# A long split-precision transformer kernel: eight units after the first and after the last RMS norm multiply unscaled tiles, and their results are scaled in the PSUM bank

## The chip, the cores and the metric

One NeuronCore of a Trainium2 chip runs the whole program. The metric is the device time of one execution in microseconds (us). Engines: TensorE (PE in the profile; PEld is its weight load), VectorE (DVE), ScalarE (ACT), GpSimd (POOL), SyncE (SP, which here issues every DMA).

## The reference

Input x is 256 tokens by 1024 features, f32. A first block is followed by two layers of a second kind:

```python
# first block
h = rms_norm(x, norm_mix_g); proj = h @ w_in            # 8192 columns
# eight attention heads, four differential heads, a gated linear recurrence,
# three gates; each branch through its own matrix, gated, summed
x = x + merged @ w_out
x = x + ffn(rms_norm(x, norm_ffn_g))                    # 2 * 2816 columns, conv, gelu
x = rms_norm(x, final_norm_g)
# then, twice
proj = x @ w_in_2[l]                                    # pool, q, k, v, conv, gates
x = layer_norm(ALPHA * x + merged @ w_o_2[l]); x = layer_norm(ALPHA * x + ffn(x))

def rms_norm(x, g):
    return x * rsqrt(mean(x * x, -1) + 1e-6) * g
```

The root depends on the token alone, the gain g on the feature alone. Features lie on the partitions here, so g is a column operand, and 1/root has to be a row that is the same on every partition.

## The kernel before

All activations are kept transposed: a tile is 128 features by S = 256 tokens, and x has KT = 8 tiles. A **unit** is one block of 128 output columns: its weight is 128 x 1024 (eight 128 x 128 blocks). f32 precision is kept by splitting: ScalarE writes `whi` (`hi_part`, line 716), VectorE writes `wlo` = raw - whi (`lo_part`, line 1372), and in `product_of` (lines 1048 to 1050) TensorE makes three matmuls for each block, whi x xhi, whi x xlo, wlo x xhi: 24 in a unit. Weights come by DMA into a ring of RING = 3 slots (`load`, line 499, on SP, which waits until the slot's `wlo` has been made). A unit's result lies in one of three banks, `unit_bank[r % 3]`, and `begin` waits until the result three before has been read (`FREE`).

The order on each engine is written out by hand. Stage `win1` has 64 units; after unit n ScalarE copies its bank to SBUF (lines 900, 897, 906), and `steps(n)` issues `hi_part(n + 3)`, on VectorE `lo_part(n + 3)`, and the small steps that `schedule` puts in slot n: `prepare_*` (tiny VectorE work), `rg_gates`, `rg_scan`, `scores` (DVE line 1541, softmax on ACT line 798), `weights` (transposes on PE line 1200, copy on ACT line 810), `values` (PE line 1220). The engines run their own lists in order and meet only at semaphores. After win1 come merge1, wout1, up1, down1, then per layer win2, wout2, up2, down2.

The two norms in question:

- The first (`first_rms`, `rms("mix", ...)`). Squares of x on ACT (line 765) and DVE (line 1453), sums over tiles on POOL (`add_squares`, line 644), sums over partitions on PE (`token_sums`, line 1105), root on ACT (line 727), reciprocal and diagonal on DVE (lines 1386, 1381), spread to all partitions by a matmul with ones (`spread_out`, line 1111). Then DVE makes the scaled tiles `dev` (line 1409), ACT `xhi` (line 758), DVE and POOL `xlo` (lines 1376, 650), and `ramp` lets units 0 and 1 start tile by tile. PE fills waits with `warm`, matmuls on ones (line 1064).
- The final (`rms("final", ...)`), after the last unit of down1 and before win20: the same, with squares made during down1 (line 931) from the residual (line 1691), `x` scaled in place.

Of the kernel before, what the change touches and what calls it, by code (L numbers as in the profile page):

```python
# [10 lines left out]
S = 256  # L11
# [13 lines left out]
RING = 3  # L25
# [6 lines left out]
PLAN1 = sum([[t, 24 + t] for t in range(KT)], []) + list(range(8, 24)) + list(range(32, WIN1))  # L32
# [102 lines left out]
def schedule():  # L135
# [5 lines left out]
    for n, name in enumerate(("prepare_scalars", "prepare_exps", "prepare_series", "prepare_sum", "prepare_softplus")):  # L141
        at(1 + n, name)
    for t in range(KT):
        at(6 + 2 * t, "rg_gates", t)
    at(22, "rg_roots",)
    for t in range(KT):
        at(23 + t, "rg_input", t)
        at(24 + t, "rg_scan", t)
        at(48 + t, "rg_hidden", t)
        at(49 + t, "rg_split", t)  # L150
    for half in range(NQT):
        at(21 + half, "turn_v", 0, half)
        at(33 + half, "turn_v", 1, half)
# [12 lines left out]
    for h in range(DIFF_H):  # L166
        at(53 + 2 * h, "diff_spread", h)
        at(54 + 2 * h, "diff_norm", h)
        at(55 + 2 * h, "diff_low", h)
    for l in range(LAYERS2):  # L170
        b = START[f"win2{l}"]
        at(b + 2, "rope", l, 0)
        at(b + 3, "turn_v2", l)
        for i in range(4):
            at(b + 4 + i, "rope", l, 1 + i)
        for pair in range(4):
            w = MOBA_H + DIFF_H + 8 * l + 2 * pair
            at(b + 9 + 4 * pair, "scores", MOBA_H // 2 + DIFF_H + 4 * l + pair)
            for i in range(2):
                at(b + 12 + 4 * pair + i + (pair == 2), "weights", w + i)  # L180
            at(b + 14 + 4 * pair + (pair == 2), "values", w)
# [10 lines left out]
SLOTS = schedule()  # L192


def build(nc, args, out):
# [3 lines left out]
    with ctx:  # L199
# [69 lines left out]
        def cst(name, n):  # L269
# [12 lines left out]
        load_vec, load_const, load_rg, load_pos, load_ident = (  # L282
            sem(n) for n in ("load_vec", "load_const", "load_rg", "load_pos", "load_ident"))
# [13 lines left out]
        normed_dve, normed_act, x_hi, x_lo, x_lo_pool = (sem(n) for n in ("normed_dve", "normed_act", "x_hi", "x_lo", "x_lo_pool"))  # L297
# [122 lines left out]
        def bank_of(r):  # L420
            return unit_bank[r % 3]

# [35 lines left out]
        FIRST_SUMMED = KT - 2  # L458
        ACCQ = {n: FIRST_SUMMED - 1 + (KT - 2) * (i - 1) if i else 0 for i, n in enumerate(NORMS)}
# [4 lines left out]
        POOL_LOW = (4, 6)  # L464
# [10 lines left out]
        for n in NORMS:  # L475
            for t in range(KT):
                if n not in LNI:
                    NORMED[n, t] = tell(normed_dve)
                elif n == NORMS[-1]:
                    NORMED[n, t] = tell(normed_dve if dve_last(t) else normed_act)  # L480
                if n != NORMS[-1]:
                    LOW[n, t] = tell(x_lo_pool if n not in LNI and t in POOL_LOW else x_lo)
# [7 lines left out]
        def _(sp):  # L490
            for i in range(KT // 2):
                sp.dma_start(x[:, 2 * i:2 * i + 2, :], args["x"][:, 2 * i:2 * i + 2, :]).then_inc(load_x[i], 16)
            def load(n, it=0, per=0):
# [18 lines left out]
            sp.dma_start(rgw[:], args["rg_w"]).then_inc(load_rg, 16)  # L512
# [1383 lines left out]
```

## Time and profile before

| what | us |
|---|---|
| median of 3 runs | 1244.67 (1243.55 to 1249.49) |
| the profiled execution | 1243.38 |
| its span in the trace | 1241.6 |
| PE busy | 1216.5 |
| DVE, ACT, POOL busy | 851.7, 706.1, 400.0 |

The span is what the trace covers; the 1.8 us beside it lie around it. A row of the timeline is: start, duration (of a merged run: of the whole), engine, line, operation, output<-input, shapes, count, and in brackets the engine's idle time before it with what ended that. Starts of consecutive rows give the pace; durations of pipelined matmuls overlap. Rows of the windows give busy time and number of instructions per engine, and PEclk, the clock that TensorE was granted (1.00 is 2.4 GHz, 0.50 is 1.2 GHz).

### The profile page before, as it was taken

To read this page: it belongs to the slowest core of one execution; us is meant where nothing else is said; L and a number is where in the kernel's file an instruction comes from. 1 tells how busy PE (TensorE), PEld (TensorE's weight loads), DVE (VectorE), ACT (ScalarE), POOL (GpSimd) and SP (SyncE) were. 2 spreads that over 40 slices of the span, in tenths; PEclk is the share of its full clock that TensorE was granted. 3 is DMA by queue.
4 is the path that set the end of the run, shared out by engine and by line. 5 is a ranking of instruction groups with operands and counts; after the bars stand their busy time and mean duration, and the time that the engine had idled before them with its cause. 6 is when DMAs were issued, how large, how long until landed. Compare 5 with 4: busy or idle time off the path is not lost. (4 is left out here: it accounts for less than half of the span.)

```text
span 1241.6 us, 27228 instructions
## 1 busy us (share of the span) xinstructions
PE 1216.5 (98%) x10224; PEld 1192.8 (96%) x10224; DVE 851.7 (69%) x1458; ACT 706.1 (57%) x1228; POOL 400.0 (32%) x376
## 2 busy tenths in 40 slices
PE   8999999999999999999999999999999999999997
PEld 8998889999999999999999999999999999999997
DVE  6858665676777755766667777756766677777755
ACT  5676666545766654466445666644466445666642
POOL 2007204023343401210338443314610339343313
PEclk9999999999999999999999999999999999999999
DMA  7554445655665666454554666664554554665662
GB/s 257 187 160 150 132 136 153 189 187 154 181 190 187 191 192 179 153 164 144 186 171 135 184 186 189 184 187 155 153 169 148 177 175 131 187 188 187 192 193 88
DMA packets 60288, 212.70 MB, mean 171 GB/s; under 512 B 6688, under 2 KB 7968, under 8 KB 60064
## 3 DMA queue, kind: packets, MB, share of 16 engines
q1 hardware_dynamic: 60192, 211.39, 55.8%
q8 instruction: 65, 1.06, 0.4%
q14 instruction: 31, 0.25, 0.1%
HBM read 210.31 MB, written 1.05 MB: 170 GB/s over the span
## 5 line engine op out<-in xcount | busy, mean ns | idle before, releaser
L1372 DVE TENSOR_TENSOR wlo<-raw,whi 128x1024 fp32r<-128x1024 f32 (+1 forms) x400 | 493.8, 1235 | 298.7 <-ACT whi L716 296.2
L1048 PE MATMUL bank<-xhi,whi 128*128 128x256 f32 x2240 | 636.6, 284 | 6.0 <-DVE wlo L1372 3.6
L1049 PE MATMUL bank<-xlo,whi 128*128 128x256 f32 x2240 | 624.4, 279 | 0.0
L1050 PE MATMUL bank<-xhi,wlo 128*128 128x256 f32 x2240 | 624.4, 279 | 0.0
L716 ACT ACTIVATE whi<-raw 128x1024 fp32r<-128x1024 f32 (+1 forms) x400 | 415.7, 1040 | 154.1 <-PE bank L1050 148.2
L1048 PEld LDWEIGHTS bank<-xhi,whi 128*128 128x128 f32 x2240 | 421.8, 188 | 16.5 <-issue 7.2
L1049 PEld LDWEIGHTS bank<-xlo,whi 128*128 128x128 f32 x2240 | 422.6, 189 | 0.6
L1050 PEld LDWEIGHTS bank<-xhi,wlo 128*128 128x128 f32 x2240 | 422.2, 188 | 0.0
L617 POOL TENSOR_TENSOR fprod<-ugate,uval 128x256 f32<-128x256 f32 x66 | 93.3, 1414 | 212.1 <-DVE uval L1717 206.5
L1048 PE MATMUL bank<-fhi,whi 128*128 128x256 f32 x528 | 148.0, 280 | 0.0
L1050 PE MATMUL bank<-fhi,wlo 128*128 128x256 f32 x528 | 147.7, 280 | 0.0
L1049 PE MATMUL bank<-flo,whi 128*128 128x256 f32 x528 | 147.6, 280 | 0.0
L631 POOL TENSOR_TENSOR u<-u,tmp 128x256 f32<-128x256 f32 x48 | 53.6, 1117 | 240.4 <-DVE tmp L1672 239.2
L1048 PE MATMUL bank<-yhi,whi 128*128 128x256 f32 x384 | 108.4, 282 | 0.0
L1050 PE MATMUL bank<-yhi,wlo 128*128 128x256 f32 x384 | 107.8, 281 | 0.0
L1049 PE MATMUL bank<-ylo,whi 128*128 128x256 f32 x384 | 107.8, 281 | 0.0
L1050 PEld LDWEIGHTS bank<-fhi,wlo 128*128 128x128 f32 x528 | 100.4, 190 | 0.0
L1049 PEld LDWEIGHTS bank<-flo,whi 128*128 128x128 f32 x528 | 99.4, 188 | 0.1
L1048 PEld LDWEIGHTS bank<-fhi,whi 128*128 128x128 f32 x528 | 99.1, 188 | 0.1
L976 ACT ACTIVATE fhi<-fprod 128x256 f32 (+1 forms) x66 | 27.6, 418 | 81.0 <-POOL fprod L617 81.0
L1048 PEld LDWEIGHTS bank<-yhi,whi 128*128 128x128 f32 x384 | 72.8, 189 | 0.3
L1050 PEld LDWEIGHTS bank<-yhi,wlo 128*128 128x128 f32 x384 | 73.0, 190 | 0.0
(201 smaller groups left out, 1287.8 us busy)
## 6 DMA issues: line engine op xcount, KB each, us to landing
raw<-in_w_win SPq DMA_DIRECT2D x140, 512.0 KB, 3.6
raw<-in_w_up SPq DMA_DIRECT2D x132, 512.0 KB, 3.6
raw<-in_w_down SPq DMA_DIRECT2D x48, 448.0 KB, 3.6
raw<-in_w_merge SPq DMA_DIRECT2D x32, 512.0 KB, 4.1
raw<-in_w_out SPq DMA_DIRECT2D x24, 512.0 KB, 3.5
raw<-in_w_down SPq DMA_DIRECT2D x24, 512.0 KB, 3.5
x<-in_x SPq DMA_DIRECT2D x4, 256.0 KB, 3.9
rgw<-in_rg_w SPq DMA_DIRECT2D x1, 1024.0 KB, 10.0
```

The costliest lines, as they stand in the source:

```text
L617: pool.tensor_tensor(tile(fprod, t % 3), tile(ugate, t % 3), tile(uval, t % 3), ALU.mult).then_inc(product, 1)
L631: ins = pool.tensor_tensor(m, m, branch_part(base, t, branch), ALU.add)
L716: act.activation(whi[:, n % RING, 0:blocks * P], raw[:, n % RING, 0:blocks * P], ACT.Copy).then_inc(split_hi, 1)
L976: act.activation(tile(fhi, t, it, 3), tile(fprod, t % 3), ACT.Copy).then_inc(f_hi, 1)
L1048: pe.matmul(ps, whi[:, slot, w], hi, start=first, stop=False)
L1049: pe.matmul(ps, whi[:, slot, w], lo, start=False, stop=False)
L1050: return pe.matmul(ps, wlo[:, slot, w], hi, start=False, stop=last)
L1372: dve.tensor_tensor(wlo[:, n % RING, w], raw[:, n % RING, w], whi[:, n % RING, w].bitcast(f32), ALU.subtract) \
```

## The change

RAW_UNITS = 8 units of win1 and of win20 no longer wait for the norm. They multiply x times the gain (`raw_high` on ACT, `raw_low` on DVE, into free halves of yhi and ylo); when the root is known, `copy_inverse` puts the spread row in SBUF and `scale_raw` on DVE multiplies each of the eight results in its bank, before ACT copies it (`unit_ready`). Three more banks (`SPARE`: ps_score, ps_turn, ps_stat) hold results 3 to 5. The sums go through PE after unit 2 (first norm) or unit 0 (final), the spread after the next unit. The scaled tiles are still made, by `normal`, `norm_hi`, `low_part`, `gained_low`, and in the first norm partly on POOL, between those units, for unit 8 on. `hi_part`/`lo_part` of units 3 to 5 (first) and 3, 4 (final) are issued ahead, and `AHEAD` says where the others go. POOL adds all eight square tiles. The first loads come in another order, with the gain column alone first. The order of win1's units changes (columns of the recurrence now begin at unit 8), and `schedule` moves nearly every small step of win1: prepare 1..5 to 7..11, rg_gates from 6 to 12, rg_roots 22 to 27, scores from every third unit from 25 to every second from 29, the differential heads' values from one unit after their weights to two. In win20 the rope steps come four units later, the attention steps one.

The diff, cut to its core:

```diff
-PLAN1 = sum([[t, 24 + t] for t in range(KT)], []) + list(range(8, 24)) + list(range(32, WIN1))
+RAW_UNITS = 8
+PLAN1 = list(range(8)) + sum([[24 + t, 8 + t] for t in range(KT)], []) + list(range(16, 24)) + list(range(32, WIN1))
...
-    at(22, "rg_roots",)
+        at(12 + 2 * t, "rg_gates", t)
+    at(27, "rg_roots",)
...
-        at(25 + 3 * pair, "scores", pair)
+        at(29 + 2 * pair, "scores", pair)
         for i in range(2):
-            at(27 + 3 * pair + i, "weights", 2 * pair + i)
-        at(29 + 3 * pair, "values", 2 * pair)
+            at(31 + 2 * pair + i, "weights", 2 * pair + i)
+        at(33 + 2 * pair, "values", 2 * pair)
     for h in range(DIFF_H):
-        at(36 + 2 * h, "scores", MOBA_H // 2 + h)
-        at(39 + 2 * h, "weights", MOBA_H + h)
-        at(40 + 2 * h, "values", MOBA_H + h)
-    at(47, "rg_gelu",)
-    at(48, "diff_sums",)
-    at(49, "diff_recip",)
+        at(37 + 2 * h, "scores", MOBA_H // 2 + h)
+        at(40 + 2 * h, "weights", MOBA_H + h)
+        at(42 + 2 * h, "values", MOBA_H + h)
...
+AHEAD = {0: 0, 1: 0, 2: 4, 3: 4, 4: 4, 5: 0, START["win20"]: 0, START["win20"] + 1: 0}
...
+        RAW_STAGE = {"mix": "win1", "final": "win20"}
+        GAIN = {"mix": "norm_mix_g", "final": "final_g"}
+        RAWI = {n: i for i, n in enumerate(RAW_STAGE)}
+        SPARE = {RESULT[name] + i: (ps_score, ps_turn, ps_stat)[i - 3] for name in RAW_STAGE.values() for i in range(3, 6)}
+        raw_xhi, raw_xlo = yhi[:, 0:KT, :], ylo[:, 0:KT, :]
+        inverse_rows = tmp[:, 2, :]
+        def bank_of(r, it=0):
+            if isinstance(it, int) and r in SPARE:
+                return SPARE[r]
             return unit_bank[r % 3]
+        def raw_units(which, i, it=0):
+            return which in RAWI and i < RAW_UNITS and isinstance(it, int)
...
+        ADDS = {n: KT - 1 if n in RAWI else KT - 2 for n in NORMS}
+        ACCQ = {n: sum(ADDS[m] for m in NORMS[:i]) for i, n in enumerate(NORMS)}
...
+            sp.dma_start(vec[:, 0:KT], args["vec"][:, 0:KT]).then_inc(load_gain, 16)
+            for i in (0, 1):
+                load_pair(i)
             load(0)
+            for i in (2, 3):
+                load_pair(i)
+            load(1)
             sp.dma_start(ident, args["const"][:, 0:P]).then_inc(load_ident, 16)
-            sp.dma_start(vec[:], args["vec"]).then_inc(load_vec, 16)
-            for n in range(1, RING):
+            load(2)
+            load(3)
+            sp.dma_start(vec[:, KT:], args["vec"][:, KT:]).then_inc(load_vec, 16)
+            for n in (4, 5):
...
+            pool.wait_ge(inverse_copied, 1)
+            for t in range(4, KT):
+                pool.tensor_tensor(dev[:, t, :], x[:, t, :], inverse_rows, ALU.mult).then_inc(normed_pool, 1)
             low_parts("mix", dev)
...
+            def raw_high(which, t, it=0):
+                if which != "mix":
+                    wait(act, res_new, RES[which] + t + 1, it, 2)
+                act.activation(tile(raw_xhi, t, it, 2), tile(x, t, it, 2), ACT.Copy, scale=gained(which, t, it)).then_inc(raw_hi, 1)
+            def copy_inverse(which):
+                act.wait_ge(spread, SUM[which])
+                act.activation(inverse_rows, spread_inverse, ACT.Copy).then_inc(inverse_copied, 1)
+            def unit_ready(which, i, n, it=0, per=0):
+                if raw_units(which, i, it):
+                    act.wait_ge(raw_scaled, RAW_UNITS * RAWI[which] + i + 1)
+                else:
+                    wait(act, unit_done, n + 1, it, per)
...
+            def first_square(t):
                 act.activation(dev[:, t, :], x[:, t, :], ACT.Square).then_inc(squared, 1)
+            for half in range(2):
+                for t in range(4 * half, 4 * half + 4):
+                    if t % 2 == 0:
+                        act.wait_ge(load_x[t // 2], 16)
+                    raw_high("mix", t)
+                if half == 0:
+                    first_square(0)
+                    first_square(2)
+                hi_part(half)
+            first_square(4)
+            first_square(6)
+            hi_part(2)
+            hi_part(3)
+            hi_part(4)
             norm_root("mix", RMS_EPS)
-            hi_part(0)
-            norm_hi("mix", dev, {3: 1})
-            hi_part(2)
+            copy_inverse("mix")
+            hi_part(5)
...
+                if n < 4:
+                    norm_hi("mix", dev, (2 * n, 2 * n + 1))
...
+            hi_part(START["win20"] + 2)
             norm_root("final", RMS_EPS)
-            hi_part(START["win20"] + 2)
-            norm_hi("final", x)
+            hi_part(START["win20"] + 3)
+            copy_inverse("final")
+            hi_part(START["win20"] + 4)
...
-                if result is not None and result >= banks:
+                if result is not None and result >= banks and not (isinstance(it, int) and result in SPARE):
...
+            def rms_sums(which):
+                token_sums(square_sums, [(acc[:, 0, :], added_q, ACCQ[which] + ADDS[which])]).then_inc(summed, 1)
+            def rms_spread(which):
                 pe.wait_ge(inverted, SUM[which])
                 spread_out(spread_inverse, 1).then_inc(spread, 1)
-                warm(7, 0)
+            def raw_unit(which, i):
+                name = RAW_STAGE[which]
+                n, r = START[name] + i, RESULT[name] + i
+                sums = 2 if which == "mix" else 0
+                ready = [(raw_lo, KT * RAWI[which] + k + 1) for k in range(KT)] if i == 0 else None
+                plain(n, r, bank_of(r)[:, 0:S], ready=ready, split=(raw_xhi, raw_xlo))
+                if i == sums:
+                    rms_sums(which)
+                if i == sums + 1:
+                    rms_spread(which)
...
+            def scale_raw(which, i):
+                n, ps = START[RAW_STAGE[which]] + i, bank_of(RESULT[RAW_STAGE[which]] + i)[:, 0:S]
+                if i == 0:
+                    dve.wait_ge(inverse_copied, RAWI[which] + 1)
+                dve.wait_ge(unit_done, n + 1)
+                dve.tensor_tensor(ps, ps, inverse_rows, ALU.mult).then_inc(raw_scaled, 1)
+                dve.wait_ge(raw_scaled, RAW_UNITS * RAWI[which] + i + 1)
+            def gained(which, t, it=0):
+                a = COLS[GAIN[which]] + t
+                return vec[:, a:a + 1] if isinstance(it, int) else vec[:, bass.ds(it * 2 + a, 1)]
+            def raw_low(which, t, it=0):
+                wait(dve, raw_hi, KT * RAWI[which] + t + 1, it, 2)
+                dve.scalar_tensor_tensor(tile(raw_xlo, t, it, 2), tile(x, t, it, 2), gained(which, t, it), tile(raw_xhi, t, it, 2).bitcast(f32),
+                                         ALU.mult, ALU.subtract).then_inc(raw_lo, 1)
...
+                    raw_low("mix", t)
+                if half == 0:
+                    first_square(1)
+                    first_square(3)
+                lo_part(half)
+            first_square(5)
+            first_square(7)
+            lo_part(2)
+            lo_part(3)
+            lo_part(4)
             dve.wait_ge(load_ident, 16)
-            rms("mix", "norm_mix_g", dev, 0, (6, 1))
-            lo_part(2)
+            invert("mix")
...
+                    scale_raw("mix", n)
+                    if n < 2:
+                        normal("mix", dev, (2 * n, 2 * n + 1))
+                    if n == 0:
+                        lo_part(5)
+                    if n in (3, 4):
+                        for t in (2 * n - 2, 2 * n - 1):
+                            gained_low("mix", t)
...
+                    invert("final")
+                    lo_part(START["win20"] + 3)
+                    lo_part(START["win20"] + 4)
...
+                        scale_raw("final", p)
+                        if p < 4:
+                            normal("final", x, (2 * p, 2 * p + 1))
+                        if 1 <= p <= 4:
+                            for t in (2 * p - 2, 2 * p - 1):
+                                low_part("final", t, x)
```

## Rows read from the trace of the kernel before

**Rows 1.** The page: busy time of each engine over the span.
```profile
PE 1216.5 (98%) x10224; PEld 1192.8 (96%) x10224; DVE 851.7 (69%) x1458; ACT 706.1 (57%) x1228; POOL 400.0 (32%) x376
```
**Rows 2.** PE's waits over the span: waited for, us in total, times, longest.
```profile
PE bank L1220 <- ACT probT L810: 4.4, 5, 1.2
...
PE bank L1200 <- DVE prob L1566: 1.5, 2, 0.9
```
**Rows 3.** Timeline of the start: warm-up, weight 0 issued, last x, first product.
```profile
0.98 6.04 PE L1064 MATMUL bank<-ones 128*128 128x128 f32 x36 [0.98 <-POOL ones L542]
...
2.59 0.43 SPq L499 DMA_DIRECT2D raw<-in_w_win  x1
...
7.94 0.43 DVE L1453 TENSOR_TENSOR dev<-x 128x256 f32<-128x256 f32 x1 [1.57 <-DMA x<-in_x]
...
15.24 0.37 PE L1048 MATMUL bank<-xhi,whi 128*128 128x256 f32 x1
```
**Rows 4.** DMA issues of the window 2.5 to 3.0: KB, us to landing.
```profile
raw<-in_w_win SPq DMA_DIRECT2D x1, 512.0 KB, 6.6
```
**Rows 5.** Timeline of PE: the starts of units 2 and 3.
```profile
22.70 0.28 PE L1048 MATMUL bank<-xhi,whi 128*128 128x256 f32 x1
...
25.42 0.28 PE L1048 MATMUL bank<-xhi,whi 128*128 128x256 f32 x1
```
**Rows 6.** Windows: busy (x) of PE, PEld, DVE, ACT, POOL; PEclk, DMA, GB/s.
```profile
7.00:8.00 1.00, 0.02 (x1) 0.00 (x0) 0.06 (x1) 0.06 (x1) 0.76 (x2) 1.00 0.94 347
...
12.00:13.00 1.00, 1.00 (x4) 0.82 (x4) 1.00 (x2) 0.00 (x0) 0.00 (x0) 0.50 1.00 404
13.00:14.00 1.00, 1.00 (x7) 1.00 (x7) 1.00 (x3) 0.55 (x2) 0.00 (x0) 0.50 1.08 437
```
**Rows 7.** DVE's groups by form: line, tiles, count, busy us, mean ns.
```profile
L1372 DVE TENSOR_TENSOR wlo<-raw,whi 128x1024 fp32r<-128x1024 f32 x352 | 440.1, 1251 | 267.1 <-ACT whi L716 265.1 <-DVE soft L1503 0.3
...
L1566 DVE TENSOR_SCALAR prob<-prob,small 128x256 f32<-128x256 f32 x28 | 10.7, 381 | 0.0
...
L1409 DVE SCALAR_TENSOR_TENSOR dev<-x,vec,bank 128x256 f32<-128x256 f32 x16 | 7.1, 478 | 0.8 <-PE bank L1111 0.8
...
L1541 DVE CUSTOM_DVE_ANT_0 prob<-bank,table 128x256 f32<-128x256 f32 x16 | 6.7, 419 | 0.0
L1605 DVE TENSOR_TENSOR_SCAN u<-u 128x256 f32<-128x256 f32 x8 | 6.7, 833 | 0.0
...
L1616 DVE TENSOR_TENSOR tmp<-bank,rope_cs 128x256 f32<-128x256 f32 x10 | 4.2, 417 | 0.0
...
L1392 DVE TENSOR_TENSOR dev<-dev,fprod 128x256 f32<-128x256 f32 x4 | 3.8, 954 | 0.0
```
**Rows 8.** ACT's groups by form.
```profile
L716 ACT ACTIVATE whi<-raw 128x1024 fp32r<-128x1024 f32 x352 | 370.1, 1052 | 102.4 <-PE bank L1050 99.9 <-DMA raw<-in_w_down 2.3
...
L900 ACT ACTIVATE u<-bank 128x256 f32<-128x256 f32 x32 | 12.1, 377 | 20.7 <-PE bank L1050 20.7
```
**Rows 9.** Windows of units 25 to 31 (scan and scores), columns as in Rows 6.
```profile
95.00:105.00 10.00, 9.39 (x82) 8.73 (x82) 8.94 (x19) 6.73 (x15) 9.64 (x11) 1.00 0.51 157
105.00:115.00 10.00, 9.09 (x78) 7.95 (x77) 9.52 (x22) 5.03 (x14) 9.42 (x10) 1.00 0.56 159
```
**Rows 10.** PE's waits from 145 to 185 us (differential heads).
```profile
PE bank L1220 <- ACT probT L810: 2.7, 3, 1.2
```
**Rows 11.** Timeline of the final norm, to the start of the third unit.
```profile
490.68 0.61 PE L1064 MATMUL bank<-ones 128*128 128x128 f32 x4
490.88 0.42 DVE L1691 SCALAR_TENSOR_TENSOR x<-x,bank 128x256 f32<-128x256 f32 x1
...
491.42 0.38 PE L1105 MATMUL bank<-ones,acc 128*128 128x1 f32 x2
...
492.50 1.14 PE L1064 MATMUL bank<-ones 128*128 128x128 f32 x8
...
493.70 0.70 PE L1111 MATMUL bank<-fprod,ones 128*128 128x256 f32 x2
494.24 1.95 PE L1064 MATMUL bank<-ones 128*128 128x128 f32 x16
...
496.19 0.36 PE L1048 MATMUL bank<-xhi,whi 128*128 128x256 f32 x1
...
501.92 0.28 PE L1048 MATMUL bank<-xhi,whi 128*128 128x256 f32 x1
```

More of the change, by code:

```diff
@@ L181, in schedule @@
-            at(b + 14 + 4 * pair + (pair == 2), "values", w)
+                at(b + 12 + late + 4 * pair + i + (pair == 2), "weights", w + i)
+            at(b + 14 + late + 4 * pair + (pair == 2), "values", w)
         at(b + 14, "pool_sums", l)
@@ L477, in build @@
                 if n not in LNI:
-                    NORMED[n, t] = tell(normed_dve)
+                    NORMED[n, t] = tell(normed_pool if n == "mix" and t >= 4 else normed_dve)
                 elif n == NORMS[-1]:
@@ L481, in build @@
                 if n != NORMS[-1]:
-                    LOW[n, t] = tell(x_lo_pool if n not in LNI and t in POOL_LOW else x_lo)
+                    LOW[n, t] = tell(x_lo_pool if n not in LNI and t in POOL_LOW[n] else x_lo)
         def square_place(t, it):
@@ L646, in low_parts @@
             def low_parts(which, src):
-                for t in POOL_LOW:
+                for t in POOL_LOW[which]:
                     pool.wait_ge(*NORMED[which, t])
@@ L652, in add_squares @@
             def add_squares(which):
-                for t in range(FIRST_SUMMED if which == "mix" else KT - 1):
+                for t in range(ADDS[which] + 1):
                     if which == "mix":
@@ L693, in _ @@
             add_squares("final")
-            low_parts("final", x)
             for l in range(LAYERS2):
@@ L751, in norm_shift, with norm_hi @@
                         .then_inc(normed_act if last else x_hi, 1)
-            def norm_hi(which, src, after={}):
-                for t in range(KT):
-                    if t in after:
-                        hi_part(after[t])
+            def norm_hi(which, src, tiles=range(KT)):
+                for t in tiles:
                     act.wait_ge(*NORMED[which, t])
-                    act.activation(xhi[:, t, :], src[:, t, :], ACT.Copy).then_inc(x_hi, 1)
+                    if which == "mix" and t >= 4:
+                        act.activation(xhi[:, t, :], src[:, t, :], ACT.Copy, scale=col(GAIN[which], t)).then_inc(x_hi, 1)
+                    else:
+                        act.activation(xhi[:, t, :], src[:, t, :], ACT.Copy).then_inc(x_hi, 1)
@@ L883, in steps @@
                     STEPS[name](*a)
-                if n < last:
-                    hi_part(n + 3)
+                if n < last and AHEAD.get(n, 3):
+                    hi_part(n + AHEAD.get(n, 3))
                 for name, *a in late:
@@ L952, in wout @@
                     for u in due:
+                        if which in RAWI:
+                            raw_high(which, u)
                         square(which, u)
+                if which in RAWI:
+                    raw_high(which, KT - 1)
                 square(which, KT - 1)
@@ L1026, in _ @@
                     steps(n, first + MIX2)
+                    if l == 0 and p < 4:
+                        norm_hi("final", x, (2 * p, 2 * p + 1))
                     if waiting is not None:
@@ L1322, in _ @@
             pe.wait_ge(ones_set, 1)
-            first_rms("mix")
-            ramp(0, 0, lows("mix"), LATER)
+            warm(20, 0)
             for n in range(WIN1):
-                if n > 1:
-                    plain(n, n, bank_of(n)[:, 0:S])
+                if n < RAW_UNITS:
+                    raw_unit("mix", n)
+                else:
+                    plain(n, n, bank_of(n)[:, 0:S], ready=lows("mix") if n == RAW_UNITS else None)
                 if n == 12:
@@ L1650, in steps @@
                         STEPS[name](*a)
-                if n < last:
-                    lo_part(n + 3)
+                if n < last and AHEAD.get(n, 3):
+                    lo_part(n + AHEAD.get(n, 3))
                 for name, *a in SLOTS.get(n, []):
@@ L1703, in wout @@
                     residual(name, t, START[name] + t, alpha, bank_of(RESULT[name] + t))
+                    if which in RAWI and t:
+                        raw_low(which, t - 1)
                 if which in LNI:
                     deviation(which, KT - 1)
+                elif which in RAWI:
+                    raw_low(which, KT - 1)
             def up(f, name, cols, width):
@@ L1740, in body @@
                         residual(name, t, n, alpha, down_bank(name, t), it, 6, 2)
+                    if which not in LNI and i % 3 == 1 and not (isinstance(it, int) and i < 3):
+                        raw_low(which, t - 1, it)
                 repeat(dve, name, DOWN, 6, body, peel_first=True)
```

136 lines of the change are left out of this document (83 added, 53 removed).

## The prediction

> **What bounds the kernel.** I read the page first: PE is busy 98% of the span, no other engine above 69% [rows 1]. So time is won only where PE doesn't make products, and lost wherever something new makes it wait. Then the list of what PE waited for: over the whole span its waits come to about 14 us, most in the attention steps [rows 2]. Neither view shows the norms, because PE fills them with matmuls on ones, which count as busy. For these I read the timeline. At the start the first product begins at 15.24 [rows 3]; units 0 and 1 end, and unit 2 begins, at 22.70, and a unit without stalls takes 25.42 - 22.70 = 2.72 us [rows 5], so the start costs what a clean start at 22.70 - 5.44 = 17.26 would. At the final norm products stop at 490.68 and the third unit begins at 501.92 [rows 11]; two units are worth 5.66 us (the ramp itself, 5.73, holds its slow first matmuls), so 5.6 us are lost. These 17.3 and 5.6 us are all that the change can shorten directly.
>
> **First norm, what is gained.** Unit 0 now needs x's tiles split and weight 0 in both parts, no root. Weight 0 was issued fifth and landed 2.59 + 6.6 = 9.2 [rows 3, 4]; the fourth transfer, the last of x, landed at 7.94 [rows 3]. In the new order weight 0 is the fourth but twice as large: I take 8.5, bounds 7.9 and 9.2. Then `hi_part(0)` 1.05 [rows 8] and `lo_part(0)` 1.25 [rows 7]: PE starts at 10.85. Tiles 4 to 7 are split by VectorE behind `lo_part(0)`, four operations with about 0.38 from start to start, ending at 12.3; unit 0 reaches its last block, seven eighths of 2.72 in, at 13.2, so they are hidden. Gain 17.26 - 10.85 = 6.4.
>
> **What is put back on PE.** Sums: eight small matmuls took 492.50 - 491.42 = 1.1 us [rows 11], four take 0.5. Spread: 494.24 - 493.70 = 0.55 [rows 11]. Together 1.05. The root chain (sums to spread 493.70 - 492.50 = 1.2 [rows 11]) is hidden by the unit between them.
>
> **The clock.** The warm-up of 36 matmuls ended at 7.0 [rows 3]; PE then idled to 9.0, and from 12 to about 15 it was granted 0.50, 1.2 GHz [rows 6]. That stretch covered warm-up matmuls. Now the warm-up has 40 and ends near 7.5, the idle time lasts to 10.85, and a stretch of some 3.2 us at the half clock would lie on units 0 and 1: half of it, 1.6 us, is lost. Bounds 0 and 1.6; I take 1.6, since the idle time is longer than the one before which it happened. The Trainium skill (TensorE: Matmul & The Clock Gate, "What you observe") calls the throttled clock the default state, which activity releases, and adds that the start differs from run to run; by it the loss may also be 0, a rival below.
>
> **The chain of banks.** This is the part that I think decides. PE takes 2.72 a unit, but units 2 to 7 now hang in one ring: `scale_raw(n)` on DVE, ACT's copy of n, `hi_part(n + 4)` behind it, `lo_part(n + 4)` on DVE, and behind that `scale_raw(n + 1)`. Starts follow by 0.45 (0.42 [rows 7] and the wait on itself) + 0.28 (the copy lasts 0.38 [rows 8], the next begins earlier) + 1.08 [rows 8] + 1.14 (of 1.25 [rows 7]) = 2.95. And it starts late. Unit 0 runs 10.85 to 13.6, units 1 and 2 to 19.0, sums to 19.5, unit 3 to 22.2, the spread lands at 22.9 (all before the clock's 1.6). Copy of the row: 23.3. DVE then has scale 0, two `normal` (0.4 each from start to start [rows 7]) and `lo_part(5)`, which ends at 25.9; unit 4 ended at 25.5, so 0.4 is lost. Scale 1, two `normal` and scale 2 end at 27.5, ACT copies and makes `whi` of unit 6 by 28.8, DVE its `wlo` by 30.1, scale 3 and its copy end at 30.85, and `begin` of unit 6 waits for just that copy (result 6 - 3). Unit 5 ended at 28.6: 2.25 are lost. Units 7 and 8 lose 0.2 each. In the catch-up the `prepare` steps (about 1.6 us of tiny DVE work each) and the convolutions of the recurrence (three operations at 0.48, 1.45) fall on the same engine that is still behind: unit 10 loses 0.15, unit 11 0.9, unit 15 0.5. Sum 4.6. GpSimd's products and low parts lie beside this. Nothing in the trace writes a bank from DVE. The nearest row reads one, 0.42; the slowest product of two 128 x 256 tiles took 0.95 [rows 7]. I take 0.42, as that row too has one operand in a bank; at 0.95 each round grows by 0.53, six rounds in each norm, 6.4 us in all. At the other end, if the ring has no cover to lose, 0.
>
> First norm: 6.4 - 1.05 - 1.6 - 4.6 = -0.8, a small loss.
>
> **Moved steps in win1.** The scores now come every two units, not three, beside the same eight scans. DVE's work for a pair of heads and two units: two `wlo` 2.4, two scans 1.7 [rows 7], scores of two heads 1.9 (0.42 and 0.28 for each, with small ones), two weights 1.8 with one reciprocal and two products each, one low part 0.4: 8.2, against 8.4 on PE (two units 5.5, steps 2.9). It was 9.5 of 10 busy here already, with GpSimd at 9.4 to 9.6 beside it [rows 9], and PE waited 1.5 us for the weights [rows 2]. Followed engine by engine, PE waits about 1 us at each of the four pairs: 4 us, 2.5 more than before. Bounds 0 and 14. Against this, the differential heads' values come two units after their weights, so that the wait for `probT`, 2.7 us in three times [rows 10], goes away. Net +0.2. In units 27 and 28 ACT has the roots and the turned values together; PE had slack there, I take 0.
>
> **Final norm.** Unit 0 of win20 starts at 490.68. Its last block comes at 493.2; tile 7 is ready earlier: residual to 491.3 [rows 11], `raw_high` to 491.7, `raw_low` to 492.2. GpSimd's last sum ends about 493.5, with the unit. Sums and spread 1.05. Row copied at 498.0; `hi_part` and `lo_part` of unit 4 stand before scale 0 on both engines, which begins at 500.1. `wlo` of unit 5 follows scale 2 and six operations on tiles at 506.6; PE wants it at 506.1. Units 6 to 8 lose 0.1 to 0.3 each, as the ring's 2.95 is hardly above 2.83. Lost 1.2; gain 5.6 - 1.05 - 1.2 = 3.3. The raw splits in down1 (0.8 us in 8.5 on ACT and DVE, each about half idle there) cost nothing; without that cover they would cost 8 times 0.8. Rope and attention steps of win20, one to four units later, I take at 0.
>
> **Sum.** The profiled execution has span 1241.6 and time 1243.38; 0.8 - 0.2 - 3.3 = -2.7 gives 1240.7. The median of the runs is 1.3 higher: 1244.67 - 2.7 = 1242.0.
>
> **Rivals.** Within 0.5%, 6.2 us, a measurement of this kernel can't tell a change from none.
> - *The queues keep up.* No half clock on products, no stalls in the ring: 6.4 - 1.05 + 0.2 + 4.5 = 10.1, 1234.6; with no more crowding of the scores 1232. For it: DVE is 69% busy overall. Against it: its order is in turns with ACT, and 2.95 is above 2.72. Chance 0.20.
> - *Only the half clock misses the products*: 1240.4. By the page's words on the start it may. 0.12.
> - *The crowded scores slow it.* Each pair adds DVE's 8.2, up to 2.0 of sharing with GpSimd and two waits for exponentials of 0.9: 12 against 8.4, 3.6 at four pairs, 14 instead of 4: 1252. It decides above 3.2 us a pair. Against it: the same mix with three units lost only 1.5. 0.07.
> - *The norms give nothing*: the ring eats both gains (scale at 0.7 or so): 1245 or a little more. 0.09.
> - *As worked out*: 0.52.
>
> The first and a tail of the others lie below 1238.4: faster 0.23; slower 0.07; the same 0.70. Range 1235 to 1248: up to the scale's dear price, down to the first rival.
>
> **What would show it.** First product at 10 to 11.5; PEclk 0.50 somewhere in 11 to 16 with products in it; a gap on PE of 2 us before unit 6, released by ACT's copy of unit 3; PE waits for `prob` over 3 us, for `probT` under 2. At 490 no break but sums and spread. The prediction is wrong if PE's products run on through units 5 to 8, or if scale_raw takes far from 0.42.

## The result and the profile after

The changed kernel takes 1259.15 us in the median of 7 runs (1254.28 to 1263.2), the kernel before 1246.15 beside it (1243.55 to 1249.49): ratio 1.0101, 95% interval 1.0081 to 1.0121. It is slower by 13 us, where 1242.0 and a range up to 1248 were forecast. The profiled execution took 1263.2, some 4 us above its median; the one of before [rows 1] took 1243.38, some 3 below its own. So the traces differ by 19.8 us, the kernels by 13; what is known of the rest stands in the last section.

The page of after, busy time of each engine (before: [rows 1]), and then what PE waited for over the span (us in total, times, longest; before: [rows 2]):

```profile
PE 1220.3 (97%) x10166; PEld 1194.2 (95%) x10166; DVE 870.5 (69%) x1486; ACT 714.2 (57%) x1246; POOL 412.0 (33%) x383
```
```profile
PE bank L1137 <- DVE wlo L1471: 8.5, 8, 3.0
PE bank L1316 <- ACT probT L880: 4.8, 3, 2.0
PE bank L1296 <- DVE prob L1715: 3.6, 3, 1.8
PE bank L1264 <- DVE tmp L1762: 3.2, 1, 3.2
PE bank L1256 <- ACT u L856: 2.3, 1, 2.3
PE bank L1137 <- ACT u L970: 2.3, 1, 2.3
PE bank L1296 <- DVE prob L1712: 1.9, 4, 0.8
```

DVE has 19 us more work and its share has not moved: the page alone shows nothing wrong. The list of waits does. Three waits of over 2 us are new, for a copy (L970), for a turned value (L856) and for the rope's product (L1762). To see where the time went, stage by stage, here are the first products of each stage in the timelines (us):

| profiled run | unit 0 of win1 | merge1 starts | down1 lasts | its end to first merge of win20 |
|---|---|---|---|---|
| before | 15.24 | 233.34 | 62.2 | 101.4 |
| after | 10.97 | 241.26 | 64.4 | 107.6 |

Unit 0 starts 4.3 earlier, yet merge1 starts 7.9 later. Down1 loses 2.2, and win20 with its norm 6.2: together 16.3 of the 19.8. The stages between and behind have the same code in both kernels.

Timeline of the start (before: [rows 3]): weight 0's wlo, first product, GpSimd's last four additions of squares, sums, first scaling, and the gap before unit 6.

```profile
9.63 1.29 DVE L1471 TENSOR_TENSOR wlo<-raw,whi 128x1024 fp32r<-128x1024 f32 x1 [1.24 <-ACT whi L748]
...
10.97 0.39 PE L1137 MATMUL bank<-yhi,whi 128*128 128x256 f32 x1 [2.95 <-DVE wlo L1471]
...
12.62 8.46 POOL L674 TENSOR_TENSOR acc<-acc,dev 128x256 f32<-128x256 f32 x4 [1.11 <-ACT dev L821]
...
21.14 0.60 PE L1193 MATMUL bank<-ones,acc 128*128 128x1 f32 x4 [1.24 <-POOL acc L674]
...
25.57 0.43 DVE L1519 TENSOR_TENSOR bank<-bank,tmp 128x256 f32<-128x256 f32 x1 [2.74 <-ACT tmp L806]
...
30.92 0.28 PE L1139 MATMUL bank<-yhi,wlo 128*128 128x256 f32 x1
33.50 0.55 PE L1137 MATMUL bank<-yhi,whi 128*128 128x256 f32 x1 [2.30 <-ACT u L970]
33.86 0.41 PE L1138 MATMUL bank<-ylo,whi 128*128 128x256 f32 x1
```

Most of this is as forecast: first product at 10.97 (10.85 forecast), `scale_raw` 0.43, a gap of 2.6 before unit 6, held by ACT's copy of unit 3. One wait was not: the sums stand 1.24 us behind GpSimd's additions, four in 8.5 us. Behind the gap products follow by 0.2 to 0.36, not 0.11. The windows show why (us, busy of PE, PEld, DVE, ACT, POOL, PEclk, DMA, GB/s; before: [rows 6]):

```profile
30.00:35.00 5.00, 2.70 (x18) 2.53 (x17) 3.28 (x5) 3.92 (x8) 3.18 (x4) 0.82 0.48 143
35.00:40.00 5.00, 5.00 (x39) 5.00 (x39) 3.79 (x7) 2.44 (x6) 0.00 (x0) 0.84 0.73 221
...
525.00:530.00 5.00, 1.80 (x13) 1.63 (x12) 3.50 (x7) 1.33 (x2) 0.00 (x0) 0.81 0.52 167
530.00:535.00 5.00, 5.00 (x25) 5.00 (x25) 1.48 (x2) 1.60 (x3) 4.07 (x3) 0.51 0.41 134
```

A part of 30 to 40 ran at the half clock (0.50, 1.2 GHz): (0.18 + 0.16) x 5 = 1.7 us of PE's full speed. The forecast had this 1.6 us, on units 0 and 1; here it sits behind the gap. Whether it costs anything there is told in the last section.

Timeline of the final norm (before: [rows 11]) and the place where win20 loses most.

```profile
501.11 0.28 PE L1137 MATMUL bank<-yhi,whi 128*128 128x256 f32 x1
...
503.93 0.50 PE L1193 MATMUL bank<-ones,acc 128*128 128x1 f32 x4
...
507.21 0.59 PE L1199 MATMUL bank<-fprod,ones 128*128 128x256 f32 x2
...
510.35 0.42 DVE L1519 TENSOR_TENSOR bank<-bank,tmp 128x256 f32<-128x256 f32 x1
...
522.59 0.42 DVE L1519 TENSOR_TENSOR bank<-bank,tmp 128x256 f32<-128x256 f32 x1
522.61 0.59 PE L1272 MATMUL bank<-u,const 128*128 128x256 f32 x2
...
524.48 1.23 DVE L1471 TENSOR_TENSOR wlo<-raw,whi 128x1024 fp32r<-128x1024 f32 x1 [1.47 <-ACT whi L748]
525.63 0.43 DVE L1519 TENSOR_TENSOR bank<-bank,tmp 128x256 f32<-128x256 f32 x1
527.52 1.23 DVE L1471 TENSOR_TENSOR wlo<-raw,whi 128x1024 fp32r<-128x1024 f32 x1 [1.47 <-ACT whi L748]
528.66 0.42 DVE L1762 TENSOR_TENSOR tmp<-bank,rope_cs 128x256 f32<-128x256 f32 x1
...
529.22 0.66 PE L1264 MATMUL bank<-const,u 128*128 128x128 f32 x2 [3.20 <-DVE tmp L1762]
529.78 0.43 DVE L1519 TENSOR_TENSOR bank<-bank,tmp 128x256 f32<-128x256 f32 x1
```

Products run on through the norm, interrupted only by the sums and the spread. Then read the two brackets of 1.47: from one `scale_raw` to the next (L1519, 522.59 and 525.63) 3.04 us go by, and for half of it DVE waits for `whi`. So it doesn't catch up with PE, which takes 2.8 for a unit. PE did the first rope step's matmul behind unit 6, at 522.61 (L1272); DVE reads its bank only at 528.66 (L1762), and until then the single bank that these small steps share (`ps_misc`) can't take `turn_v2`. PE stands for 3.2 us, and 530 to 535 run at the half clock, which takes 2.5 us of full speed more.

Timeline of ACT in down1, and PE's wait that answers to it:

```profile
444.79 0.95 ACT L748 ACTIVATE whi<-raw 128x896 fp32r<-128x896 f32 x1 [1.52 <-PE bank L1139]
447.81 0.51 ACT L802 ACTIVATE yhi<-x,vec 128x256 fp32r<-128x256 f32 x1 [2.07 <-DVE x L1837]
448.34 1.28 ACT L850 ACT_TABLE_LOAD   x1
...
450.38 1.28 ACT L767 ACT_TABLE_LOAD   x1
...
451.91 1.06 ACT L748 ACTIVATE whi<-raw 128x1024 fp32r<-128x1024 f32 x1
...
454.37 0.38 PE L1137 MATMUL bank<-fhi,whi 128*128 128x256 f32 x1 [1.90 <-DVE wlo L1471]
```

`raw_high` (L802) itself costs 0.51. But it waits 2.07 for the residual. The sines and the root's table (two table loads of 1.28) stand behind it in ACT's queue, and the next `whi` behind these; PE waits 1.9 for the `wlo` made from it.

### The profile page after: what moved, and what is told of

It is laid out like the page before. It is cut to its first block and busy times, and to the rows that moved or that the text cites. A ratio compares the mean times of both kernels' runs of the same rounds, so it can differ in the third digit from the quotient of the medians.

```text
span 1261.4 us, 27194 instructions
## 1 busy us (share of the span) xinstructions
PE 1220.3 (97%) x10166; PEld 1194.2 (95%) x10166; DVE 870.5 (69%) x1486; ACT 714.2 (57%) x1246; POOL 412.0 (33%) x383
## 3 DMA queue, kind: packets, MB, share of 16 engines
q8 instruction: 64, 1.05, 0.4%
HBM read 210.31 MB, written 1.05 MB: 168 GB/s over the span
## 5 line engine op out<-in xcount | busy, mean ns | idle before, releaser
L1137 PE MATMUL bank<-xhi,whi 128*128 128x256 f32 x2112 | 603.7, 286 | 4.6 <-DVE wlo L1471 3.0
L1138 PE MATMUL bank<-xlo,whi 128*128 128x256 f32 x2112 | 591.9, 280 | 0.0
L1139 PE MATMUL bank<-xhi,wlo 128*128 128x256 f32 x2112 | 591.8, 280 | 0.0
L1138 PEld LDWEIGHTS bank<-xlo,whi 128*128 128x128 f32 x2112 | 399.3, 189 | 0.6
L1137 PE MATMUL bank<-yhi,whi 128*128 128x256 f32 x512 | 145.7, 285 | 7.1 <-DVE wlo L1471 3.6
L1138 PE MATMUL bank<-ylo,whi 128*128 128x256 f32 x512 | 143.6, 280 | 0.0
L1139 PE MATMUL bank<-yhi,wlo 128*128 128x256 f32 x512 | 143.5, 280 | 0.0
L1137 PEld LDWEIGHTS bank<-yhi,whi 128*128 128x128 f32 x512 | 97.5, 190 | 8.8 <-DVE wlo L1471 8.4
L1139 PEld LDWEIGHTS bank<-yhi,wlo 128*128 128x128 f32 x512 | 97.4, 190 | 0.0
L1138 PEld LDWEIGHTS bank<-ylo,whi 128*128 128x128 f32 x512 | 96.9, 189 | 0.1
```

What stands on the lines that cost most here:

```text
L1137: pe.matmul(ps, whi[:, slot, w], hi, start=first, stop=False)
L1138: pe.matmul(ps, whi[:, slot, w], lo, start=False, stop=False)
L1139: return pe.matmul(ps, wlo[:, slot, w], hi, start=False, stop=last)
```

## The experiments

Each is the changed kernel with the edit named; ratios are to the kernel before, run beside it (medians 1244.3 to 1245.2). "Less" means less than the changed kernel, by the difference of the two ratios. By the two intervals such a difference is uncertain by 3 to 5 us, so the medians alone show only the larger ones (8.7, 5.7 and 7.6 below); for the smaller ones the argument rests on waits and stage times in the traces.

### The final norm taken back

```diff
-        RAW_STAGE = {"mix": "win1", "final": "win20"}
+        RAW_STAGE = {"mix": "win1"}
```
(and down1, the final norm and win20's slots as before)

> The changed kernel with the raw units of the final norm taken back: down1, the final norm, win20 and their steps are as before, the first norm and win1 stay as changed. Theory A, the loss sits in both stages, each by steps that meet a late VectorE: the trace of the changed kernel loses 6.2 us between the end of down1 and the first merge of win20, so this kernel should stand near 1259.2 - 6.2 = 1253, and its wait for turn_v2 (3.2 us) and the half clock behind it (about 2.5 us) should be gone. Rival B, all the loss comes from win1 and its moved scores, and the final norm costs nothing: 1258 to 1260. Rival C, the first norm and win1 cost nothing: 1246 to 1248.

1247.94 us (10 runs), ratio 1.0031 (1.0015 to 1.0046). The final norm's part is 1.0101 - 1.0031, some 8.7 us, more than the 6.2 of win20: down1's 2.2 belong to it too, which theory A had left out, so that its 1253 was missed. By the ratio the first norm and win1 cost 3.9 us (1.9 to 5.7). So the loss sits in both stages, as A has it. B is out; the time lies in C's range, but C's cause, that the first norm and win1 cost nothing, does not hold against the kernel before beside it.

### Ropes behind the raw units

```diff
-        at(b + 2 + late, "rope", l, 0)
-        at(b + 3 + late, "turn_v2", l)
...
+            for i, s in enumerate((8, 9, 10, 12, 13)):
+                at(b + s, "rope", l, i)
+            at(b + 11, "turn_v2", l)
```

> The changed kernel with the five rope steps and turn_v2 of win20 in slots 8, 9, 10, 12, 13 and 11 of the stage, not 6, 8 to 11 and 7: behind the last unit whose result is scaled. Theory A, VectorE is some 6 us behind TensorE while results are scaled, and only steps that meet it there cost: the wait of 3.2 us and the half clock behind it (about 2.5 us) go, 1253.5. Rival, VectorE is late for whatever comes and the wait moves to the first scores or to the weights: 1257 to 1260.

1259.05, ratio 1.0122 (1.0092 to 1.0152): nothing gained, the rival is right. Unit 8 of win20 now starts 24.6 after down1's end, not 28.4, and most of that is lost again by the first merge (106.2, not 107.6). PE's waits between down1 and the first merge:

```profile
PE bank L1276 <- DVE tmp L1766: 2.6, 2, 2.3
PE bank L1320 <- ACT probT L884: 2.0, 1, 2.0
PE bank L1276 <- ACT u L865: 1.5, 1, 1.5
PE bank L1141 <- DVE wlo L1475: 1.4, 2, 0.7
...
```

With two small ones they sum to 8.4, against 7.3 in the changed kernel's stage. The new waits (L1276) are those of rope steps in consecutive slots for the bank that they share.

### Scores every third unit

```diff
-        at(29 + 2 * pair, "scores", pair)
+        at(28 + 3 * pair, "scores", pair)
```
(weights 30, values 32 + 3 * pair; the differential heads 2 later)

> The changed kernel with the eight heads' scores in win1 every third unit again (28, 31, 34, 37, not 29, 31, 33, 35) and the differential heads two units later, their values still two units behind their weights. Theory A, the crowding costs what the trace shows over what the old spacing cost: waits of 0.5, 0.3, 1.9 and 2.3 us and about 1.3 us of half clock, against 1.5 us before: 5 us less, 1254. Rival, the waits only move to the differential heads, which now end later: 1258 to 1260.

1254.46, ratio 1.0074 (1.005 to 1.0099), 3.4 less, and merge1 starts at 234.16, not 241.26. PE's waits from 106 to 200 in it, and, behind, in the changed kernel (before: [rows 2, 10]):

```profile
PE bank L1296 <- DVE prob L1715: 3.6, 3, 1.8
PE bank L1296 <- DVE prob L1712: 1.8, 2, 1.4
```
```profile
PE bank L1296 <- DVE prob L1715: 3.6, 3, 1.8
PE bank L1256 <- ACT u L856: 2.3, 1, 2.3
PE bank L1316 <- ACT probT L880: 1.9, 1, 1.9
PE bank L1296 <- DVE prob L1712: 0.8, 2, 0.5
```

From unit 29 to merge1 it takes 128.3 us here (pair 0's score matmuls, 0.86, which now lie ahead of unit 29, are added). The changed kernel took 134.7, five other kernels with its win1 132.1 to 133.8. The kernel before took 128.4, if its unit 29 is put at 91.30 + 5 x 2.72 (unit 24's start, with all gates and turns done). So the crowding costs 4 to 6 us, and this edit takes all of it back.

### whi ahead of the copy

```diff
+                if 2 <= n < RAW_UNITS and AHEAD.get(n, 3):
+                    hi_part(n + AHEAD.get(n, 3))
                 unit_ready("mix", n, n)
```
(the same in win20; the calls behind the copy are left out for these units)

> The changed kernel with one order turned round in units 2 to 7 of both raw stages: ScalarE makes whi of the unit ahead before it copies the scaled result, so that hi_part no longer stands behind scale_raw. Theory A, the ring of scale, copy, whi, wlo (3.05 us a round in the trace, against 2.72 to 2.85 on TensorE) is what keeps VectorE behind: it is cut, VectorE catches up within the raw units, the gap before unit 6 falls from 2.6 to about 1 us, the wait for turn_v2 falls under 0.5 us and both half-clock stretches go: 1251 to 1253. Rival, VectorE's own work is the limit, not the order: 1257 to 1260.

1252.83, ratio 1.0055 (1.0036 to 1.0075), 5.7 less. In win20 unit 8 starts 26.7 after down1's end, not 28.4, and the wait for `turn_v2` is 1.6, not 3.2. In win1 the gap before unit 6 stays at 2.3: whi of unit 7 now stands ahead of the copy that unit 6 waits for. Behind the gap the ring is faster: unit 12 starts 17.0 after unit 6, not 18.2. So theory A has the time right and the ring, but not the gap, and the wait for `turn_v2` is not under 0.5. The trace shows about 1 us in each stage: unit 12 at 49.2, not 50.1 to 51.7, and 106.5 from down1's end to the first merge, not 107.6. It has no half clock on products before 585; part of the 5.7 may be that, so the order alone may be worth less.

### Raw results not scaled

```diff
-                dve.tensor_tensor(ps, ps, inverse_rows, ALU.mult).then_inc(raw_scaled, 1)
...
-                    act.wait_ge(raw_scaled, RAW_UNITS * RAWI[which] + i + 1)
+                wait(act, unit_done, n + 1, it, per)
```

> The changed kernel without scale_raw: the sixteen raw results are not multiplied by the inverse root, and ScalarE copies each as soon as its unit is done; roots, spread, row copy and scaled tiles are still made. This prices the chain behind scale_raw. Theory A, the ring scale, copy, whi, wlo keeps VectorE some 6 us behind and so makes the gap before unit 6, the waits in win20's first half and the half clock behind them: all of these go, 8 to 10 us, 1249 to 1251. Rival, only the operation's own 16 times 0.45 us leaves an engine that is not the limit, and the late root is what holds VectorE: 1256 to 1259.

This kernel leaves the scaling out. 1248.89, ratio 1.004 (1.0022 to 1.0057), 7.6 less, as theory A has it, for 16 operations of 0.43. The waits for `turn_v2` and for the copy are gone; those of the second half of win20 (2.1, 2.0, 0.6) are not. So `scale_raw` with the chain behind it is a large cause, and not the only one.

### gated_conv moved with its neighbours

```diff
-            at(b + 17 + 4 * t, "gated_conv", l, t)
+            at(b + 17 + late + 4 * t, "gated_conv", l, t)
```
(pool_sums and pool_mix too)

> The changed kernel with win20's two gated_conv steps, pool_sums and pool_mix one unit later too, so that all steps of its second half stand to each other as in the kernel before. Theory A, the attention steps, which moved by one unit alone, meet gated_conv on VectorE and ScalarE: the three waits that all kernels with raw units in win20 show 52 to 65 us after its scores begin (0.6, 0.3 and 2.0 us, against one of 0.8 before) fall to about 0.8, so 2 us less: 1257. Rival, those waits come from VectorE's delay in the raw units and not from the shift: 1259.

1255.55, ratio 1.0073 (1.0047 to 1.0098); the gain, 3.5 us, is uncertain by as much, but the waits between down1 and the first merge are plain:

```profile
PE bank L1264 <- DVE tmp L1762: 3.2, 1, 3.2
PE bank L1296 <- DVE prob L1712: 1.7, 1, 1.7
PE bank L1316 <- ACT probT L880: 0.9, 1, 0.9
PE bank L1137 <- DVE wlo L1471: 0.4, 1, 0.4
```

Of the three waits at the end (0.6, 0.3 and 2.0) one of 0.9 is left, as before. From down1's end to the first merge it takes 104.5, not 107.6.

### The bank's true holder

```diff
+                    back = 6 if banks == 3 and isinstance(it, int) and result - 3 in SPARE else banks
-                    done, count = FREE[result - banks + ahead]
+                    done, count = FREE[result - back + ahead]
```

> The changed kernel in which units 6 to 8 of both raw stages wait for the copy of the result that really was in their bank (six before, since results 3 to 5 lie in spare banks), not for the one three before. Theory A, the gap of 2.6 us before unit 6 of win1 has two holders close together: without the copy of unit 3 the unit waits for its own wlo, ready 0.9 us earlier in the trace, so it saves about 1 us and 1258 comes out. Rival, the bank is the only holder: 2.5 us and 1.5 of half clock saved, 1255.

1259.01, ratio 1.009 (1.0058 to 1.0123). Unit 6 waits 1.46 for its wlo where it waited 2.30 for the copy, 0.8 less, as theory A has it. But nothing is left of it a little later: unit 12 starts at 50.15, and at 50.07 in the run with the ropes moved, whose unit 6 waits for the copy. So the 0.8 could not show in the time, and the median doesn't show it.

### First norm alone, repaired

The final norm taken back, with scores every third unit, whi first and the bank's true holder.

> Raw units in the first norm alone (as in the run that took the final norm's back, 1247.9), with three repairs together: scores every third unit, whi ahead of the copy in units 2 to 7, and the relaxed wait for the bank. Theory A, the repairs add up, since they mend different gaps: -3.4 for the scores (as measured), about -2 for the order and -1 for the bank: 1241 to 1243, some 3 us under the kernel before. Rival, the start's 6 us can't be kept whatever is mended, because the later gap only moves: 1245 to 1247.

1241.26 (12 runs), ratio 0.9971 (0.9957 to 0.9984): 3.6 us faster than the kernel before, and in theory A's range. Merge1 starts at 230.67, against 233.34 before.

### Sines first in down1

```diff
                     elif not (isinstance(it, int) and i < 3):
+                        if i == 3 and isinstance(it, int) and name == "down1":
+                            step_prepare_sines()
+                            load_sqrt()
                         if i % 3 == 0:
```

> The changed kernel in which ScalarE, in the first units of down1, makes the sines and reloads the root's table before the first raw_high, as it did in the kernel before, and not behind it. In the trace the first raw_high waits for the residual and holds both table loads (1.28 us each) back, and TensorE waits 1.9 us for the wlo behind them. Theory A: that wait goes, and with it 1.9 us, 1257. Rival, the 1.9 us are made up later in down1, or a DMA is what holds there: 1259.

1255.12, ratio 1.0087 (1.0063 to 1.0111). PE has no wait in down1 any more. The size, 1.7, agrees with 1.9; the interval alone would not show it. Down1's time does: it takes 60.9 here, and 62.6 in the run with the bank's true holder, which has the wait and whose products follow at the same pace in this stage.

### Everything mended

(the edits named above, six of the final norm's low parts on GpSimd, and new slots for win20's ropes)

> Both norms raw, with every repair: those of the run with raw units in the first norm alone (1241.3), the sines first, whi before the copy in win20 too, the low parts of six of the final norm's tiles on GpSimd (idle there), ropes of win20 in slots 5, 7, 11, 12, 13 and turn_v2 in 9, so that two of them never follow within a unit, and gated_conv and the pool steps one unit later with the attention steps. Theory A, the final norm's gain of 3.3 us was real and was only eaten by VectorE's delay and the steps that met it: 1241.3 - 3.3 = 1238, at most 1239.5. Rival, a late root always costs the final norm what it saves, whatever is mended: 1241 to 1244.

1240.03 (10 runs), ratio 0.9966 (0.9948 to 0.9983), between theory A's 1239.5 and the rival's 1241. Down1's end to the first merge is 98.9, against 101.4 before: 2.5 of the forecast 3.3 are there. Between this run and the one without a raw final norm (0.9971) the medians don't decide, so in the time of the whole kernel a gain of the final norm is not shown. Several edits are new in this run at once; what each is worth was not tested. PE's waits in the stage are 2.0 for a rope step behind DVE's read and 0.8 for `probT`.

### The changed kernel's rope slots in it

> The same with the rope steps and turn_v2 left in the changed kernel's slots (6, 8 to 11, and 7). Theory A: what VectorE is late by decides; with whi first and six low parts off it the delay is under a unit by slot 7, the waits for turn_v2 and rope stay under 1 us and it comes out within 1 us of the run before. Rival, two steps in one bank within a unit cost a wait of 1.5 to 2.5 us anyway: 2 us slower than that run.

1241.86 (12 runs), ratio 0.9978 (0.9962 to 0.9994), not told apart from the run before. The ropes wait 0.37, as theory A has it, but the weights behind them 1.90; the stage takes 99.3, not 98.9.

### Two last waits

```diff
+            for i, s in enumerate((5, 7, 11, 15, 19)):
+                at(b + s, "rope", l, i)
...
+        at(43 + 2 * h, "weights", MOBA_H + h)
+        at(45 + 2 * h, "values", MOBA_H + h)
```
(everything else as in the run with everything mended, and `diff_sums` and `diff_recip` a slot later)

> The run with every repair (1240.0), and two more: win20's ropes in slots 5, 7, 11, 15 and 19 (its trace still shows TensorE waiting 1.98 us for the rope step behind turn_v2), and the differential heads' weights and values in win1 one unit later (TensorE waits there for prob in three times, 3.6 us in all). Theory A, a step costs only where it comes before its data: both waits fall under 1 us together, 1235 to 1237. Rival, each wait only moves to the next step of the same chain, as it did when the ropes alone were put later: 1239 to 1241.

1233.33 (6 runs), ratio 0.9913 (0.9886 to 0.9939): 11 us faster than the kernel before, more than the 8 to 10 expected. The rival is out. PE's waits from down1 to the first merge:

```profile
PE bank L1306 <- DVE prob L1722: 0.9, 1, 0.9
PE bank L1326 <- ACT probT L885: 0.9, 1, 0.9
```

The stage takes 97.7, 3.7 under before; merge1 starts at 228.21, 5.1 under before. Against the run with everything mended the two places give 1.2 us (win20) and 2.3 (unit 29 to merge1); in the latter the waits of the differential heads are gone, and one of 1.7 behind GpSimd (L1341) is new. By the ratios the runs differ by 6.6; what stands beyond these 3.5 is not traced to the edit.

## Why the prediction was wrong

- **The start.** Right: 10.97 for 10.85 (9.66 to 10.65 in the other twelve profiles with raw units), `scale_raw` 0.43 for 0.42, the gap before unit 6 2.6 for 2.25, its holder ACT's copy.
- **The half clock.** 1.7 us for 1.6, on other units, and there it cost nothing (last section). Of the seven profiles whose unit 6 waits 2.3 us for the copy, three show it there and four don't; on units 0 and 1 one of thirteen does (granted clock 0.66 from 10 to 15, scores every third unit). The Trainium skill (TensorE: Matmul & The Clock Gate, "What you observe") says of the passage from the slow to the fast pace that its time varies from run to run; here it also varies whether a slow stretch comes at all.
- **The first norm's sum**, -0.8. Five kernels with the changed front and the changed scores (ropes, no final norm, gated_conv, bank, sines) start unit 29 at 104.97 to 105.50, the profiled one at 106.57, before it would be 104.90: -0.1 to -0.6, here -1.7. The profiled one has the 1.24 behind GpSimd that the others don't have. In it one addition lasts from 12.62 to 17.66, while VectorE works from 12.9 to 17.1 without a gap; the shortest take 0.74. The forecast priced no wait for these additions. That the sum is right in size is partly luck. In the five the start gained 7.1 to 7.3, not 6.4, the ring and the catch-up cost 6.3 to 6.6, not 4.6 (with the forecast 1.05 for sums and spread), and the clock's 1.6 was not a cost at all.
- **Moved steps in win1**, net +0.2 forecast, measured -4 to -6. The first term, crowded scores, was near as a sum of waits: 4 us forecast, found 0.5, 0.3, 1.9 and 2.3, and half clock behind that was not forecast. The second failed wholly: "the wait for probT goes away" came true, 2.7 to 0, and its place was taken by `prob` (L1715), 0.6 before and 3.6 now. Over the span the waits for `probT` came to 4.8, where the forecast named under 2 as its sign. Scores, exponentials, weights, values are one chain; PE arrives at its next link earlier by what it no longer waits at the last. The crowding was also the only rival that made the kernel slower (0.07); it has a part of the loss, and no rival had the final norm lose.
- **Raw splits in down1 "cost nothing"**: 1.9. The sum priced eight operations on engines half idle. It had to price one wait of ACT, for the residual, and two table loads behind it. The Trainium skill (ScalarE: Activation LUTs, "What ACT_TABLE_LOAD costs") gives about 1283 ns for a load and 1380 more for a drain; the trace shows 1.28, and the next instruction at 449.63, right at its end, so the drain isn't seen here.
- **Final norm**, +3.3 forecast, measured -6.2 (-3.1 to -7.2 over the seven profiles with a raw final norm, its scaling and at most one edit). The step that failed most is the one I priced last: "Rope and attention steps of win20, one to four units later, I take at 0". I had the ring's 2.95 (3.04 measured) and its late start, and charged them only where a unit waits for a bank or a weight. But steps meet the late engine too: 3.2 at `turn_v2`, 2.5 of half clock (in this profile; of four others with the same wait three have 1.7 and one none), and 2.1 more (2.9 for 0.8) where the attention steps had moved by one unit against `gated_conv`. Moving the ropes alone gained nothing; leaving out the scaling, which makes the engine late, gained 7.6. The 3.3 itself could be had in the stage: 3.7 in the last run, with the steps moved again.
- **Readings.** PE's waits before sum to 15.6 us, not about 14, and the attention steps have 6.5 of them, not most. DVE's 9.5 of 10 [rows 9] is the second window; the first has 8.9. Neither changes the sum.

The sum in place: first norm about -0.5, win1 -4 to -6, down1 -2, win20 -6: about 13. The medians agree: 3.9 for the first two, 8.7 for the others.

## What to carry to other kernels

When a change makes one engine late by some units, list every step that comes due while it is late and price each, also those whose own code is untouched. Here a short read of a shared bank held PE longest. An operation on a half-idle engine is free only if it doesn't wait: look up what its operand comes behind, and what is queued behind it. A removed wait in a chain is a gain only as far as the next link is early.

## What the runs showed of the hardware

The pitch of products, from one start to the next, has two values under one granted clock. In the kernel before, matmuls of the same shape, PE busy all the time:

```profile
340.00:350.00 10.00, 10.00 (x91) 10.00 (x90) 7.79 (x11) 6.55 (x11) 3.56 (x3) 1.00 0.63 189
460.00:470.00 10.00, 10.00 (x87) 10.00 (x87) 5.25 (x6) 4.01 (x5) 1.47 (x1) 1.00 0.71 207
```

Starts follow by 0.113 us in the first and by 0.118 in the second, 4%, a unit in 2.72 or 2.83. Where it changes differs from execution to execution of like code: down1 without a wait takes 60.9 us in two profiles (sines first; changed rope slots) and 62.6 in a third (everything mended). Summed over all product starts less than 0.16 apart, what lies above 0.1133 was 26 us in the profile of before, 30 in after, 19.5 where the final norm was taken back and 23 in the last run. The 19.5 fit a profiled execution of 1241.69 under a median of 1247.94, though no other execution of that kernel was traced; 26 against 30 is some 4 of the 19.8 us between the first two traces. What sets it was not tested, nor whether long work without a gap brings it on, which would take back a part of any gain.

The half clock, as (1 - PEclk) x 5 over windows of 5 us inside the program, came to 5.0 us in the profile of before, 10.0 in after and 1.7 in the last run. It follows gaps of 2 to 3 us in some executions and not in others (at unit 6: 0.82 and 0.84 above, and with the ropes moved 1.00):

```profile
30.00:35.00 5.00, 3.06 (x25) 2.94 (x26) 4.45 (x8) 3.08 (x7) 1.62 (x1) 1.00 0.49 158
35.00:40.00 5.00, 5.00 (x42) 4.97 (x43) 2.98 (x5) 2.43 (x4) 0.00 (x0) 1.00 0.65 208
```

What it costs depends on whether PE sets the pace behind it. At unit 6 it costs nothing:

| profile | unit 6 | unit 12 | apart | lost to the half clock behind unit 6 |
|---|---|---|---|---|
| after | 33.50 | 51.67 | 18.2 | 1.7 |
| final norm taken back | 32.19 | 50.36 | 18.2 | 1.7 |
| sines first | 32.37 | 50.61 | 18.2 | 1.7 |
| ropes late | 31.94 | 50.07 | 18.1 | 0 |
| gated_conv moved | 32.08 | 50.25 | 18.2 | 0 |

Without the slow stretch PE waits the more for `wlo` (1.0 from 20 to 60 with the ropes late, 0.3 in after): the ring sets the pace. Elsewhere it costs a part. From unit 29 to merge1 the profiles that lose 3.4 us to it take 133.7 to 134.7 (after is the longest), those that lose none 132.1 (whi first, sines first). From down1's end to the first merge those that lose 3.4 take 107.6 (after) and 108.6 (bank's true holder, sines first), and one with like waits that loses none takes 106.2 (scores every third unit).
